# A two-block transformer forward pass on one core: splits placed ahead of casts and squares in the two embedding stages, and query lows, key copies and the compressed branch placed later in the attention's entry

## The reference

```python
    for i in range(DEPTH):
        if i < N_A:
            x = x + pool_mixer(rmsnorm(x, norm_mix[i]), pool_w[i], pool_scale[i])
        else:
            ...
            x = x + nsa_attention(rmsnorm(x, norm_mix[i]), w_in_b[j], w_out_b[j], cos, sin, kv)
        x = x + conv_ffn(rmsnorm(x, norm_ffn[i]), ffn_up[i], ffn_conv[i], ffn_conv_b[i], ffn_down[i])
        gate = jax.nn.sigmoid(rmsnorm(x, norm_ple[i]) @ ple_gate[i])
        x = x + gate * (p[i] @ ple_proj[i])
    return rmsnorm(x, norm_final)
```

## Time and profile before

| | |
|---|---|
| median of 3 runs | 3144.55 us (3144.1 to 3147.39) |
| the profiled execution's own time | 3145.3 us |
| its span, first to last instruction | 3143.5 us, 1.8 us less |
| TensorE matmul busy | 3017.3 us, 96% of the span, 13608 matmuls |
| VectorE, ScalarE, GpSimd busy | 1595.4 us (51%), 1195.0 us (38%), 525.2 us (17%) |
| chain that ended last, by engine | TensorE 83%, VectorE 9%, ScalarE 4% |
| mean granted TensorE clock | 0.983 of full |
| weight load of an embedding job, issue to landing | 640 KB, median 3.8 us |

### The profile page before, as it was taken

How to read it: one execution, slowest core, us unless ns; L and a number is a source line. 1 busy time by engine, 2 the same in 40 slices (tenths; PEclk the granted TensorE clock), 3 DMA queues, 4 the chain that set the end, 5 groups by cost and what they waited for, 6 DMA issues and landing times.

```text
span 3143.5 us, 37270 instructions
## 1 busy us (share of the span) xinstructions
PE 3017.3 (96%) x13608; PEld 2468.1 (79%) x13608; DVE 1595.4 (51%) x1838; ACT 1195.0 (38%) x1589; POOL 525.2 (17%) x517
## 2 busy tenths in 40 slices
PE   7999989979999999999999889999999998999997
PEld 6888867868788887788888678888888886788886
DVE  6665356487566634533337844333343336843323
ACT  5553233368555423322222343222322225632221
POOL 1111110235311111211101211111111112511110
PEclk9999999979999999999999989999999999999999
DMA  4222232100122222222232112222322222222222
GB/s 160 96 104 78 98 119 83 54 14 2 60 101 93 81 93 92 102 94 93 85 102 70 54 54 95 103 84 92 108 93 99 85 96 94 81 97 104 89 87 78
DMA packets 47162, 272.63 MB, mean 87 GB/s; under 512 B 5936, under 2 KB 7776, under 8 KB 24800
## 3 DMA queue, kind: packets, MB, share of 16 engines
q1 hardware_dynamic: 47072, 271.42, 24.9%
HBM read 269.29 MB, written 2.11 MB: 86 GB/s over the span
## 4 chain that ended last, share of the span: by engine, by line
PE 83%; DVE 9%; ACT 4%; issue 2%; POOL 1%; DMA 1%; SPq 0%; POOLq 0%; DVEq 0%; ACTq 0%
PE bank L483 26%; PE bank L484 26%; PE bank L485 26%; DVE w_lo L1624 2%; PE bank L779 1%; ACT w_hi L1065 1%; DVE cy L2148 1%; ACT probs L1341 1%; DVE x L1641 1%; PE bank L691 0%; DVE rs L1630 0%; PE bank L795 0%; PE bank L794 0%; DVE rc L2321 0%; POOL r_lo L2591 0%
## 5 line engine op out<-in xcount | busy, mean ns | idle before, releaser
L483 PE MATMUL bank<-h_hi,w_hi 128*128 128x512 f32 x2448 | 964.0, 394 | 24.5 <-DVE w_lo L1624 13.5
L484 PE MATMUL bank<-h_lo,w_hi 128*128 128x512 f32 x2448 | 954.9, 390 | 0.0
L485 PE MATMUL bank<-h_hi,w_lo 128*128 128x512 f32 x2448 | 954.8, 390 | 0.0
L1624 DVE TENSOR_TENSOR w_lo<-w_raw,w_hi 128x2048 fp32r<-128x2048 f32 (+2 forms) x282 | 577.7, 2048 | 576.0 <-ACT w_hi L1065 575.7
L1065 ACT ACTIVATE w_hi<-w_raw 128x2048 fp32r<-128x2048 f32 (+2 forms) x282 | 474.7, 1683 | 335.0 <-PE bank L485 306.8
L483 PEld LDWEIGHTS bank<-h_hi,w_hi 128*128 128x128 f32 x2448 | 460.6, 188 | 133.9 <-issue 14.4
L484 PEld LDWEIGHTS bank<-h_lo,w_hi 128*128 128x128 f32 x2448 | 460.7, 188 | 97.8 <-issue 3.4
L485 PEld LDWEIGHTS bank<-h_hi,w_lo 128*128 128x128 f32 x2448 | 460.5, 188 | 96.9
L483 PE MATMUL bank<-act_hi,w_hi 128*128 128x512 f32 x1056 | 411.7, 390 | 7.3 <-DVE hid L1753 4.7
L485 PE MATMUL bank<-act_hi,w_lo 128*128 128x512 f32 x1056 | 410.9, 389 | 0.0
L484 PE MATMUL bank<-act_lo,w_hi 128*128 128x512 f32 x1056 | 410.8, 389 | 0.0
(11 more groups left out here) (356 smaller groups left out, 3238.5 us busy)
## 6 DMA issues: line engine op xcount, KB each, us to landing
w_raw<-in_w_up SPq DMA_DIRECT2D x132, 1024.0 KB, 4.9
w_raw<-in_w_down SPq DMA_DIRECT2D x96, 704.0 KB, 4.0
w_raw<-in_w_wout SPq DMA_DIRECT2D x12, 1024.0 KB, 4.9
w_raw<-in_w_ple SPq DMA_DIRECT2D x16, 640.0 KB, 3.8
w_raw<-in_w_ein SPq DMA_DIRECT2D x6, 1024.0 KB, 4.9
w_raw<-in_w_kproj SPq DMA_DIRECT2D x4, 1024.0 KB, 4.9
w_raw<-in_w_qproj SPq DMA_DIRECT2D x4, 1024.0 KB, 4.9
w_raw<-in_w_ogate SPq DMA_DIRECT2D x4, 1024.0 KB, 4.8
```

Source lines behind the costliest of these rows:

```text
L483: pe.matmul(out, wh, mh, start=first, stop=False)
L484: pe.matmul(out, wh, ml, start=False, stop=False)
L485: return pe.matmul(out, wl, mh, start=False, stop=final)
L1624: dve.tensor_tensor(w_lo[j % 2][:, 0:n], w_raw[j % 2][:, 0:n], w_hi[j % 2][:, 0:n].bitcast(F32), ALU.subtract).then_inc(w_lo_done, 1)
```

## The change

Embedding stages. TensorE no longer begins with the stat matmul: it starts the first gate sum as soon as chunk 6 of x is added, and makes the stat matmul between the first gate sum and the first projection sum. On ScalarE and VectorE the split of job 1 now precedes the root and, on VectorE, the low parts of p; job 2 is split right after the root or reciprocal. From then on job m+2 is split behind the sigmoid of m (ScalarE) and behind the addition to x of m (VectorE), ahead of the cast, the squares and the low part of chunk m. Layer 0's `angles` follow in jobs 2 to 5; layer 1's casts go ahead of its squares and `final1` is drawn into job 7.

Attention. `key_copies` 1 and 3 and `query_los` 5, 6 and 7 leave the entry and stand in units 6 to 14 (`DEFERRED`). The maxima of unit 0 go ahead of the subtraction, those of unit 1 and the reciprocal of unit 0 ahead of the compressed sums; ScalarE's exp of `e4` comes after unit 0's; the compressed transposes and what follows them come after unit 2 instead of unit 1. `keep_half` writes to `e4`, since `qr` is now read until unit 14. The two functions at line 1956 move out unchanged, so that `attention()` can call them.

```diff
@@ -140,6 +140,7 @@
 T_ORDER = (0, 2, 3, 1)
 SLOTS = 4
+DEFERRED = {6: (5, None), 8: (None, 1), 10: (6, None), 12: (None, 3), 14: (7, None)}
 CS_BANKS = (2, 3, 4, 7)
 E_SPANS = (4 * P, 3 * P)
@@ -542,7 +543,7 @@
     stage = f"ple{l}"
-    stats(stage)
+    pe.wait_ge(x_ready, x_before(stage) + ND - 1)
         for u in range(2):
@@ -554,12 +555,14 @@
                     pe.wait_ge(h_lo_done, H_COUNT[stage] + k + 1)
             mm.then_inc(seg_done, 1)
+            if isinstance(i, int) and m == 0:
+                stats(stage)
             pe.wait_ge(acc_free, FREE0[stage] + 2 * m - 2)
             mm.then_inc(seg_done, 1)
-    pairs(pe, ND // 2, body)
+    pairs(pe, ND // 2, body, peel=1)
@@ -740,6 +743,8 @@
             pe.wait_ge(cs_vec, CS_DONE + t // 2)
                 pe.wait_ge(cs_lo, t - 1)
+            else:
+                pe.wait_ge(u_lo, 3)
             for g in range(NG):
             mm.then_inc(cs_turned, 1)
@@ -750,13 +755,15 @@
         t = T_ORDER[i]
         if u == 0 and i == 0:
-            pe.wait_ge(k_done, 8)
+            pe.wait_ge(k_done, 4)
             pe.wait_ge(k_hi_done, 16)
             pe.wait_ge(q_lo_done, s + 1)
+        if u == UNITS // 2 and i == 0:
+            pe.wait_ge(k_done, 8)
         if u >= 1:
         out = bank[t][:, 0:n]
@@ -771,8 +778,8 @@
             pe.wait_ge(u_scaled, NT * (u + 1))
             pe.wait_ge(u_lo, n - 1)
-        else:
-            pe.wait_ge(cs_lo, n + 3)
+        if n == 3:
+            pe.wait_ge(cs_lo, NT)
         for kb in USES[x]:
                 at, to = t * (t + 1) // 2 * P + kb * P, use_at(x, kb) + (t - kb) * P
@@ -828,7 +835,7 @@
             qk(u, 3)
             turn(u - 2, 2)
-        if u == 1:
+        if u == 2:
             compressed_turned()
 def even():
@@ -1171,7 +1178,6 @@
 def squares_of_both(m):
     at = 9 * PREP_OF["final1"] + 2 * m
-    act.wait_ge(x_ready, x_before("final1") + m + 1)
     act.wait_ge(sq_added, at + 1)
     act.wait_ge(sq_added, at + 2)
@@ -1197,28 +1203,31 @@
     act.wait_ge(p_loaded, 16 * (l + 1))
         act.activation(p_hi[:, k], taps_in[:, k, PAD:], ACT.Copy).then_inc(p_hi_done, 1)
+    split_w(j0 + 1)
     root(stage)
-    def body(i):
-        for u in range(2):
-            m, j = 2 * i + u, j0 + u
-            if isinstance(i, int):
-                split_w(j0 + m + 1)
-            else:
-                split_w(j + 1, 16 * ((j + 1) // 2 + 1) + 16 * i, s0 + 2 * m)
-            act.wait_ge(acc_free, FREE0[stage] + 2 * m + 1)
-            act.activation(ple_t[:, u], ple_t[:, u], ACT.Sigmoid).then_inc(sig_done, 1)
-            if l == 1:
-                squares_of_both(m)
-                if m < EARLY:
-                    hi_of_two(m)
-                continue
-            wait_x(nxt, m)
-            if l == 0:
-                act.activation(h2_hi[:, m], x[:, m], ACT.Copy, scale=col("kv", m)).then_inc(h2_hi_done, 1)
+    split_w(j0 + 2)
+    for m in range(ND):
+        u = m % 2
+        if l == 1 and m == ND - 1:
+            act.wait_ge(seg_done, s0 + 2 * m + 1)
+            hi_of_two(EARLY)
+        act.wait_ge(acc_free, FREE0[stage] + 2 * m + 1)
+        act.activation(ple_t[:, u], ple_t[:, u], ACT.Sigmoid).then_inc(sig_done, 1)
+        if 1 <= m < ND - 1:
+            split_w(j0 + m + 2)
+        if l == 0:
+            act.wait_ge(x_ready, x_before(nxt) + m + 1)
+            act.activation(h2_hi[:, m], x[:, m], ACT.Copy, scale=col("kv", m)).then_inc(h2_hi_done, 1)
+            act.wait_ge(sq_added, 9 * PREP_OF[nxt] + m + 1)
             square(nxt, m)
-    for i in range(ND // 2):
-        body(i)
+            continue
+        if m == ND - 1:
+            for later in range(EARLY + 1, ND - 1):
+                hi_of_two(later)
+        act.wait_ge(x_ready, x_before(nxt) + m + 1)
+        if m < EARLY or m == ND - 1:
+            hi_of_two(m)
+        squares_of_both(m)
     act.wait_ge(const_set, 3)
@@ -1355,16 +1364,13 @@
         act.wait_ge(head_done, s + 1)
             act.wait_ge(o_sum, s - 1)
-        act.activation(qr[s % 2][0:HD], bank[6 + s % 2][HD:P], ACT.Copy).then_inc(half_kept, 1)
+        act.activation(e4[0:HD, s % 2], bank[6 + s % 2][HD:P], ACT.Copy).then_inc(half_kept, 1)
-    for half in range(2):
-        act.wait_ge(cs_vec, CS_SHIFTED + half)
-        act.activation(e4[:, 2 * half:2 * half + 2], e4[:, 2 * half:2 * half + 2], ACT.Exp).then_inc(cs_exp, 1)
     for u in range(UNITS + 6):
         if back:
@@ -1384,7 +1390,11 @@
         if now:
             exps(u, 3)
-        if u == 1:
+        if u == 0:
+            for half in range(2):
+                act.wait_ge(cs_vec, CS_SHIFTED + half)
+                act.activation(e4[:, 2 * half:2 * half + 2], e4[:, 2 * half:2 * half + 2], ACT.Exp).then_inc(cs_exp, 1)
+        if u == 2:
             for t in range(NT):
                 act.activation(pc_hi[:, :, t * P:(t + 1) * P],
@@ -1599,10 +1609,6 @@
         attention_inputs()
         attention()
-    elif stage == "final1":
-        act.wait_ge(seg_done, SEGS_BEFORE[J0["ple1"] + ND])
-        for m in range(EARLY, ND):
-            hi_of_two(m)
     elif stage == "final2":
     elif stage in ("wout0", "wout1", "wout2"):
@@ -1811,33 +1817,33 @@
         one, two = VC["final1"], VC["ffn2"]
         dve.wait_ge(fold_set, 3)
+    split_w(j0 + 1)
     for k in range(2):
     norm_factors(stage)
-    def body(i):
-        for u in range(2):
-            m = 2 * i + u
-            split_w(j0 + u + 1 if not isinstance(i, int) else j0 + m + 1, j0 + m + 2)
-            if l == 1 and 1 <= m <= EARLY:
-                lo_of_two(m - 1)
-            if l == 0 and m:
-                key_lo(m - 1)
-            if l == 0 and m >= 3:
-                angles(m - 3)
-            dve.wait_ge(seg_done, s0 + 2 * m + 1)
-            dve.tensor_tensor(ple_t[:, u], bank[2 * u][:], rs[:], ALU.mult).then_inc(acc_free, 1)
-            dve.wait_ge(seg_done, s0 + 2 * m + 2)
-            dve.wait_ge(sig_done, ND * l + m + 1)
-            dve.tensor_tensor(ple_t[:, u], bank[2 * u + 1][:], ple_t[:, u], ALU.mult).then_inc(acc_free, 1)
-            dve.wait_ge(acc_free, FREE0[stage] + 2 * m + 2)
-            add_to_x(nxt, m, ple_t[:, u], 1.0)
-    for i in range(ND // 2):
-        body(i)
-    if l == 0:
-        key_lo(ND - 1)
+    split_w(j0 + 2)
+    for m in range(ND):
+        u = m % 2
+        dve.wait_ge(seg_done, s0 + 2 * m + 1)
+        dve.tensor_tensor(ple_t[:, u], bank[2 * u][:], rs[:], ALU.mult).then_inc(acc_free, 1)
+        dve.wait_ge(seg_done, s0 + 2 * m + 2)
+        dve.wait_ge(sig_done, ND * l + m + 1)
+        dve.tensor_tensor(ple_t[:, u], bank[2 * u + 1][:], ple_t[:, u], ALU.mult).then_inc(acc_free, 1)
+        dve.wait_ge(acc_free, FREE0[stage] + 2 * m + 2)
+        add_to_x(nxt, m, ple_t[:, u], 1.0)
+        if 1 <= m < ND - 1:
+            split_w(j0 + m + 2)
+        if l == 0:
+            key_lo(m)
+            if 2 <= m < 6:
+                angles(m - 2)
+        elif m < EARLY:
+            lo_of_two(m)
+    if l == 1:
+        for m in range(EARLY, ND):
+            lo_of_two(m)
@@ -1906,6 +1912,21 @@
 ...
+def key_copies(r):
 ...
+def query_los(c):
 ...
@@ -1956,21 +1977,6 @@
 ...
-    def key_copies(r):
 ...
-    def query_los(c):
 ...
@@ -1990,13 +1996,10 @@
         rope_start(n + 5, bank[n % 2][:])
             query_los(n - 3)
-        if n >= 4:
+        if n in (4, 6):
             key_copies(n - 4)
     query_end(6)
-    query_los(5)
     query_end(7)
-    query_los(6)
-    query_los(7)
     dve.wait_ge(gates_done, 1)
@@ -2028,9 +2031,12 @@
     both(lambda i: dve.tensor_reduce(s[i], e[i], AX, ALU.max))
     both(lambda i: dve.tensor_scalar(s[i], s[i], NEG / 10, None, ALU.max))
+    peaks_first()
     both(lambda i: dve.tensor_tensor(e[i], e[i], spread(s[i]), ALU.subtract))
     assert count == CS_SHIFTED + 1
-    peaks_first()
+    inverse(0)
+    for i in range(4):
+        peak(1, i)
     dve.wait_ge(cs_exp, 1)
     dve.wait_ge(cs_exp, 2)
@@ -2043,8 +2049,8 @@
     both(lambda i: dve.tensor_tensor(e[i], e[i], spread(f[i]), ALU.mult))
-    for u in range(UNITS + 4):
-        now, back = 1 <= u < UNITS, 2 <= u < UNITS + 2
+    for u in range(1, UNITS + 4):
+        now, back = 2 <= u < UNITS, 2 <= u < UNITS + 2
         if now:
             peak(u, 1)
@@ -2062,7 +2068,10 @@
             inverse(u)
             keep_lo(u - 2, 2)
-        if u == 1:
+        if u in DEFERRED:
+            c, r = DEFERRED[u]
+            query_los(c) if r is None else key_copies(r)
+        if u == 2:
             for t in range(NT):
                 cols = slice(t * P, (t + 1) * P)
@@ -2108,7 +2117,7 @@
     if half == 0 and c >= 2:
     dve.wait_ge(half_kept, s + 1)
-    dve.tensor_tensor(o_f[c % 2][half * HD:(half + 1) * HD], bank[6 + s % 2][0:HD], qr[s % 2][0:HD], ALU.add)\
+    dve.tensor_tensor(o_f[c % 2][half * HD:(half + 1) * HD], bank[6 + s % 2][0:HD], e4[0:HD, s % 2], ALU.add)\
         .then_inc(o_sum, 1)
 def residual(stage):
@@ -2418,9 +2427,6 @@
```

(27 more changed lines are left out.)

## The result

The kernel before took 3144.81 us (median of 4 runs, 3144.10 to 3147.39), the changed one 3123.18 us (4 runs, 3122.49 to 3124.62): a ratio of 0.9929 with a 95% interval of 0.9916 to 0.9941, so 18 to 26 us faster. Forecast were 3123 us. The profiled execution took 3122.82 us, its span 3121.0 against 3143.5.

The account below looks back on a forecast made before the run. TensorE, busy 96% of the span, was taken as the bound, so only its waits could give time. 10.7 + 14.4 + 4.2 - 7.3 = 22.0 us off 3145.3 gave 3123; range 3112 to 3134.

Parts of the forecast that it names:

- Layer 0's embedding stage: Layer 0's embedding stage: 15.7 us gained without disturbance, less 5.0 us taken back, 10.7 us gained.
- The undisturbed pace: Layer 0's embedding stage: all `w_lo` waits go, so the next stage's stat matmul comes 15.7 us earlier.
- the disturbance: Layer 0's embedding stage: GpSimd's additions and `angles` lengthen VectorE's jobs to 7.3 to 8.3 us, taking back 5.0 us.
- The collision: Embedding stages: GpSimd's addition of squares goes first, so `key_lo` or `lo_of_two` takes 1.8 us or more.
- Layer 1's: Layer 1's embedding stage: 16.4 us gained, less 2.0 us for low parts 6 and 7, 14.4 us.
- Rival 1: Embedding stages reach TensorE's pace undisturbed, GpSimd's additions slipping behind the low parts: 3114 to 3117; chance 0.22 with rival 2.
- rival 3: VectorE bounds layer 0's embedding stage, its lag carried into the keys, heavy contention in the units: 3136; chance 0.13.
- The entry: Attention's entry: deferral brings the mask step 4.5 us earlier; entry summed as 4.2 us gained, 3 to 6.
- The new order: Mask step to maxima of unit 3: reordered first units give 0, between 1.5 gained and 1.5 lost.
- The deferred pieces: Attention units: ten pieces inside the ring of VectorE and ScalarE move later units, 7.3 us lost, upper end 11.
- Rival 2: Attention units: deferred pieces are free because TensorE sets the pace, 3116; chance 0.22 with rival 1.
- Rival 4: Attention units: TensorE's clock stays at its lower level, all 30 units making 61 us lost, 3206; chance 0.02.

Follow-up runs that it names:

- experiment 5: The changed kernel, but in the embedding stages VectorE makes the low part of chunk m-1 behind the gate product of m: 3120.55 us.
- experiment 6: The changed kernel, but the deferred pieces stand as ten single halves ahead of the reciprocals of units 4 to 14, not as pairs behind `keep_lo`: 3117.36 us.

## Why the prediction was right, and where its terms were off

**Layer 0's embedding stage** (forecast 10.7, measured 11.35). The undisturbed pace was 15.7 us better by my sum; experiment 5, where TensorE no longer waits for `w_lo`, shows 77.47 - 61.59 = 15.9. For the disturbance I had 5.0, and it was 4.5, but its parts differ. The collision came as described: GpSimd starts its addition 0.1 us ahead of `key_lo`, and six of the eight take 1.78. VectorE's jobs took 7.2 to 8.1 us (7.3 to 8.3 forecast). That the collision was to blame for all of it, as I had it ("if VectorE goes first each time it is 0"), is not shown: experiment 5 left most of the collision and filled the wait for the sigmoid. The `w_lo` of job 7 was 0.22 late instead of 1.0 and that of the keys' job 0 2.05 (forecast 2.1). The last `h2_lo` and the squares were not late at all (2.0 forecast), because TensorE itself was late by then: the low clock behind the 2.05 us wait cost 7.25 - 5.44 = 1.8 us in that job. I had put this only into the pessimistic end of the range. The new wait for `p_lo` was 0.79, not 1.3; `p_lo` ahead of the split removes it, and the stage gains 1.05 us (61.59 to 60.54): the idle time and some 0.2 us more, as I had taken for the filling of the pipe.

**Layer 1's** (14.4, measured 14.58). The two late low parts were 0.70 and 0.73 (0.9 and 1.1 forecast), `p_lo` 0.9. Rival 1, no collision, is out by `key_lo`'s 1.78 us; rival 3 by the sums. An addition of 1.31 us begun 0.09 us earlier leaves 1.22, and `key_lo` took 1.04 more than its 0.74. The Trainium skill, "SBUF — State Buffer", section "SBUF: two separate sides", has the second to start, of a VectorE instruction with two SBUF inputs and a GpSimd instruction that reads SBUF, wait until the first is through. The trace agrees to within 0.18 us.

**The entry** (forecast 4.5 for the deferral). Measured 3.96, of which 0.73 are the clock of the one-column matmuls; 3.2 are the change's, and the other traces with the deferral give 3.3 to 3.9 in the same way. The removed work was 5.2 + 2.7 us, and the two uncovered waits are 1.54 and 2.16 us (1.3 and 2 forecast). What I missed is a collision that moved: the last `w_lo` split of the queries' stage, at 610.18, now meets GpSimd's work for the keys and takes 3.25 us; before it came at 625.85 and took 2.29. 7.9 - 3.7 - 1.0 is 3.2. My sum, by the way, entered 4.2 for the entry, where its own terms, 4.5 and 0, give 4.5.

**The new order** (forecast 0, between -1.5 and 1.5). It costs 1.05 us in four traces and 1.85 in the change's. In the change's trace TensorE waits 4.0 us for `keep_lo` ahead of unit 0's last transposes and another 2.5 ahead of the compressed transposes, which now stand between units 2 and 3. It looks as if that costs more than the three short waits saved behind unit 1, but the parts of the reorder were not tested singly. This term is the one that I should have given a sign: work moved out of the cover of other work has to be paid where it lands.

**The deferred pieces** (forecast 7.3 lost, measured 8.45). Right in kind: they cost more than the entry gains, each by its full length and a little more. ScalarE's first exp waits 2.1 us behind a pair of query lows and 1.6 behind a pair of copies, five times in all (1.7 and 1.1 forecast). Three pairs of query lows moved the units by 1.97 us each and two pairs of copies by 1.30: from the reciprocal at 674.94 to that at 681.66 are 6.72 us, where the same unit of the kernel before took 4.75. Short by 1.1 because I took 0.15 us of contention a piece. A pair takes 1.81 instead of 1.37, and it also stretches GpSimd's scaling, 2.92 us where the kernel before shows 2.06. The upper end, 11 us, was much too far. Rival 2, that they are free, is out by experiment 6 against this one: free only in the idle 0.9 us ahead of the reciprocal.

**Rival 4** is out: the granted clock was 1.00 in every window from 670 to 750 us, over all five deferred pairs, and the units without one kept their 4.2 us.

The sum of the change's own stretches is 11.35 + 14.58 + 3.2 - 1.85 - 8.45 = 18.8 us, or 19.6 with the 1.05 that the order cost in the other traces. By that the forecast of 22.0 was 2.4 to 3.2 too high, for the order, the deferral and the entry. The rest of the measured 21.6 us (span 22.5) comes from the start, 1.9, the rest of the program, 1.0, and the clock of the one-column matmuls, 0.7, which vary between executions. The median fell by 0.9 us less than the profiled span. That the forecast met the median to a microsecond is chance; its terms are right within 1.9 us each. Two slips stand beside the sum. I named 25 us for `up2`'s stat matmul, which leaves out the attention that lies ahead of it: it came 21.5 us earlier. And the chances of "within 0.2%", 0.03 and 0.03, make 0.06, not 0.05.

## What to carry to other kernels

When two engines wait for each other in turn, ask in whose idle time a piece of work is put. The same ten operations cost 8.45 us right ahead of what the other engine waits for, and 0.15 us just ahead of the point at which their own engine waits; a pair that doesn't fit has to be cut to the gap's size. Splitting early makes room only as long as each job of the engine that splits stays shorter than TensorE's; look for what lengthens it, a collision with another reader of SBUF as well as an idle wait in its middle, and fill the idle wait first. An operation moved out of a collision may leave it to its neighbour: look at the durations of all operations nearby, not only at the one that was moved. And test the halves of a change alone, because here a good one hid a bad one.

## What the runs showed of the hardware

Even without any wait TensorE's clock can be low, and it differs between traces of kernels whose instructions in that phase are the same. Thirty-two one-column matmuls behind 128-column ones took from 3.64 us (granted clock 1.00) to 5.93 us (0.59). Over the ten traces the two series together vary by 2.9 us, as much as several of the edits that were to be judged, and comparisons of single edits are better made stretch by stretch.

The collision of two engines goes both ways: VectorE's pair of lows lengthened from 1.37 to 1.81 us and GpSimd's four scalings from 2.06 to 2.92 in the same moment. It also meets operations with a single input in SBUF: beside GpSimd's addition the cast of the angles took 1.52 us instead of 0.41.

Taking away a wait that TensorE's rows give as 0.79 us shortened the stage by 1.05 us, and one of 0.86 us in layer 1 by 1.05 to 1.07: some 0.2 us more than the rows call idle.
